# Layernorm statistics and gate rows moved from VectorE to ScalarE in a hybrid decoder step

## The chip, the cores and the metric

The kernel runs on all 8 cores of one Trainium2 chip. Each core works on its own share: one prompt sequence of 2048 tokens and 16 decode sequences of 8 tokens. The cores do not talk to each other. The time is that of the slowest core in device microseconds; the kernel before took 947.68 us in the median of three runs (946.88 to 950.29).

## The reference, cut to what matters

One layer of a decoder trunk. `a` is the normalised input, and `w_in` is one matrix whose columns are split into the inputs of two head groups.

```python
a = rmsnorm(h, norm_mix)
u, vg, q, k, vm, o, zi, zf = jnp.split(a @ w_in, SPLITS, axis=-1)
# head group A: chunked gMLP spatial gating (4 heads x 128 channels)
u = jax.nn.gelu(u)
vg = layernorm(jax.nn.gelu(vg), gm_ln_g, gm_ln_b)      # over the 512 channels of a token
y_gm = u * (causal 128x128 position mix of vg + bias)
# head group B: mLSTM matrix memory (4 heads, dk = dv = 128), chunks of 128 tokens
ig = zi + ml_b_i ; lf = log_sigmoid(zf + ml_b_f)
b  = cumsum(lf) ; m_t = running max of (b + m, b - b_s + ig_s)
w_inter = exp(b + m - m_t) ; w_end = exp(D[last] - m_new) ; dec = exp(b[last] + m - m_new)
num, den -> h ; C, n updated
...
h = h + [y_gm | y_ml] @ w_out
h = h + relu(rmsnorm(h) @ w_up)**2 @ w_down            # 1024 -> 4096 -> 1024
h = h + sigmoid(rmsnorm(h) @ w_pg) * (p @ w_pp) ; final rmsnorm
```

`layernorm` is `(x - mean) * rsqrt(var + eps) * g + b`, where mean and variance are over the 512 gMLP channels of a token. The outputs are the tokens, the new memories and the normalised `v` rows of the last chunk.

## The kernel before

**Tiles and halves.** A core has 17 tiles of 128 tokens: 16 of the prompt and one of the 16 decode sequences (the sample tile). They are worked on in two halves. The first holds prompt tiles 0 to 7 and the sample tile, in groups of two prompt tiles (256 columns), with the sample tile as a group of its own in third place. The second holds tiles 8 to 15 in four groups. A group goes through four stages: norm (`norm_T`, L865: square with accumulation and scaling on ScalarE, eight transposes on TensorE, one 128x1024 multiplication by the gain on VectorE, here `AR<-pb,GN`), projections (`stage_P`, L894: u, v, gates, o, m, q, k), the gate chain (`stage_G`, L958) and mixing (`stage_M`, L1047: both head groups, output projection, residual). When all groups of a half are through, the half's FFN follows in four quarters (`ffn_group`, L1169; its first matmuls are 128x384, three tiles wide), and the last per-layer step and the final norm (`stage_C`, L1189) follow the last quarter. The norms and the u, o and gate projections and the gate chain of the second half's first group stand before the last third of the first half's last FFN quarter.

**Layernorm of v, in `stage_P` (L934 to L945).** For each tile ScalarE evicts gelu of the v projection into `vn` (128x512, f32). VectorE takes its statistics in one pass and folds them (`bn_stats`, `bn_aggr`), GpSimd makes the reciprocal root (`rstd`, L861: a `tensor_scalar` and a power, 128x1 each), VectorE makes minus mean times that root (`stt`), ScalarE applies both (Identity with a bias and a scale of one number per partition), and GpSimd multiplies by the gain row `GROW` and adds the bias row `BROW` (128x512 each).

**The gate chain, in `stage_G` (L958 to L1030).** The gates lie as rows: 4 heads on 4 partitions, 256 tokens along the free axis. ScalarE makes exp and ln of the forget gate and adds the input gate's bias; VectorE makes the cumulative sum (`scan` into `ROWN`), adds it to the input gate, takes the running maximum (`scan` into `ROWR`), copies its value at the chunk ends into `RSEG`, and writes three blocks of rows into the tile `ROWX`, at partitions 32, 64 and 96: segment maximum minus running maximum, cumulative sum minus running maximum, and input gate minus segment maximum. TensorE transposes `ROWX` (matmuls `pb<-IDF,ROWX`, one per tile), spreads the decay of the memory (`pb<-DCB,ONEF`), and ScalarE exponentiates what comes out (`GSM`). `stage_M` cannot begin a tile without it. Matmuls `R,OH` spread the split running maximum.

**What sets the order.** Nothing is written out by hand. `stage_P`, `stage_G` and the others only record operations with their operands; a list scheduler (`Plan.schedule`, L393) gives each engine its order from estimated durations, from the cost of handing over between engines (`CROSS`, `SAME`), of changing ScalarE's function table (`TABLE`), and from how many PSUM banks each class of tiles may hold. So an edit of a few operations can move others far away. Where the scheduler foresees that TensorE will wait, it puts matmuls that compute nothing (`pb<-BSR,ONEB`, 128x512) before the waiting operation:

```python
spare = s - free[e] - 0.9 - (4.0 if late is not None and late.dma else 0.0)
each = FILL if s > 30.0 else 2 * FILL          # FILL = 0.22
o.fill = int(spare / each) if spare > 2 * each else 0
```

A single `BSR,ONEB` followed by `WM,AR x4` is no filler but the bias of the position mix. All instructions are issued from one helper line, L252, and all DMAs from L276, so the trace tells groups apart by tile names. Weights are loaded on GpSimd's queue: the FFN quarters by `load_q` (L1162), whose first quarter overlays the place of the u and v columns of `w_in`, so it is issued once the last group's u and v projections are through.

Of the kernel before, what the change touches and what calls it, by code (L numbers as in the profile page):

```python
# [7 lines left out]
AF = mybir.ActivationFunctionType  # L8
ALU = mybir.AluOpType
# [6 lines left out]
EPS = 1e-6  # L16
# [505 lines left out]
def build():  # L522
# [35 lines left out]
    with ExitStack() as st:  # L558
# [23 lines left out]
        def act(out, in_, func, bias=None, scale=None, accum=None):  # L582
            kw = dict(out=out, in_=in_, func=func)
            if bias is not None:
                kw["bias"] = bias
            if scale is not None:
                kw["scale"] = scale
            if accum is not None:
                kw["accum_out"] = accum
            cost = 0.17 + _nelem(in_) / 1200.0 + 0.09 * nptr(bias, scale) + (0.19 if accum is not None else 0)  # L590
            return P.add("act", [("activation", kw)], aps(in_, bias, scale), aps(out, accum), cost, tset=FN.get(func))
# [6 lines left out]
        def tt(eng, out, in0, in1, op):  # L598
            n = _nelem(out)
            mode = 2 if all(_dsize(x.dtype) == 2 for x in (out, in0, in1)) else 1  # L600
            cost = vcost(eng, n, mode)
            if eng == "pool":
                cost = 0.1 + n * (0.0026 if _dsize(in0.dtype) == 4 else 0.0019) + (0.55 if op == ALU.pow else 0)
            return P.add(eng, [("tensor_tensor", dict(out=out, in0=in0, in1=in1, op=op))], [in0, in1], [out], cost)

        def ts(eng, out, in0, s1, op0, s2=None, op1=None):
            kw = dict(out=out, in0=in0, scalar1=s1, scalar2=s2, op0=op0)
            if op1 is not None:
                kw["op1"] = op1
            mode = 1 if is_ps(in0) else (4 if _dsize(in0.dtype) == 2 and _dsize(out.dtype) == 2 else 2)  # L610
            return P.add(eng, [("tensor_scalar", kw)], aps(in0, s1, s2), [out],
                         vcost(eng, _nelem(out), mode, nptr(s1, s2)))

        def stt(eng, out, in0, scalar, in1, op0, op1):
            return P.add(eng, [("scalar_tensor_tensor", dict(out=out, in0=in0, scalar=scalar, in1=in1, op0=op0,
                                                             op1=op1))],
                         aps(in0, scalar, in1), [out], vcost(eng, _nelem(out), 1, nptr(scalar)))
# [8 lines left out]
        def dve(name, out, in_, **kw):  # L626
            return P.add("dve", [(name, dict(out=out, in_=in_, **kw))], [in_], [out], vcost("dve", _nelem(in_)))
# [129 lines left out]
        XH = [A.bf(512) for _ in range(3)]  # L757
# [100 lines left out]
        def small(g, off, n):  # L858
            return SMALL[:, g % 6, off:off + n]

        def rstd(out, tmp, ss, mul, add, n=1):  # L861
            ts("pool", tmp, ss, mul, ALU.mult, add, ALU.add)
            tt("pool", out, tmp, NEGH[:, 0:n], ALU.pow)
# [30 lines left out]
        def stage_P(grp, part=0, pg=None):  # L894
            gi = cnt["g"]
            nt = len(grp)
            n = nt * 128
            at = AT[gi % 2]
            d2 = gi % 2

            def feat(nm, fin):
                w = win(nm)
                for hp in range(2):
                    p = ps("P")
                    for hh in range(2):
                        h = hp * 2 + hh
                        mm(p[:, hh * n:(hh + 1) * n],
                           [(w[:, kc, h * 128:(h + 1) * 128], at[:, kc, 0:n]) for kc in range(8)])
                    fin(p[:, 0:2 * n].rearrange("p (h t) -> p h t", h=2), slice(hp * 2, hp * 2 + 2))

            def tokm(nm, j):
                w = win(nm)
                p = ps("P")
                mm(p, [(at[:, kc, j * 128:(j + 1) * 128], w[:, kc, :]) for kc in range(8)])
                return p

            marks = []
            if part == 2:
                marks = None
            else:  # L920
                feat("u", lambda p, hs: marks.append(act(UT[d2][:, hs, 0:n], p, AF.Gelu_apprx_tanh)))
            def gates():
                pg = ps("P")
                mm(pg[:, 0:n], [(WGT[:, kc, :], at[:, kc, 0:n]) for kc in range(8)])
                return pg

            def ogate():
                feat("o", lambda p, hs: act(SGT[d2][:, hs, 0:n], p, AF.Tanh, scale=0.5))

            if part == 1:  # L930
                pg = gates()
                ogate()
                return pg
            for j, t in enumerate(grp):  # L934
                vn = VN[t["n"] % 2]
                act(vn, tokm("v", j), AF.Gelu_apprx_tanh)
                st6, mv, tm, rs = small(t["n"], 4, 6), small(t["n"], 10, 2), small(t["n"], 12, 1), small(t["n"], 13, 1)
                dve("bn_stats", st6, vn)
                dve("bn_aggr", mv, st6)
                rstd(rs, tm, mv[:, 1:2], 1.0, EPS)  # L940
                nm = small(t["n"], 14, 1)
                stt("dve", nm, mv[:, 0:1], -1.0, rs, ALU.mult, ALU.mult)
                act(vn, vn, AF.Identity, bias=nm, scale=rs)
                tt("pool", vn, vn, GROW[:], ALU.mult)
                tt("pool", XH[t["n"] % 3], vn, BROW[:], ALU.add)  # L945
                if t["ty"] == 1 or t["i"] == NPT - 1:
                    tt("pool", vn, vn, BROW[:], ALU.add)
                    dma(o_Vs if t["ty"] == 1 else o_Vp, vn)
            if part == 0:
                pg = gates()  # L950
                ogate()
            for j, t in enumerate(grp):
                cp("act", VAUG[t["n"] % 4][:, :, 0:128], tokm("m", j).rearrange("p (h d) -> p h d", h=4))
            feat("q", lambda p, hs: cp("act", QT[d2][:, hs, 0:n], p))
            feat("k", lambda p, hs: act(KT[d2][:, hs, 0:n], p, AF.Copy, scale=QK_SCALE))
            return pg, marks

        def stage_G(grp, pg):  # L958
            gi = cnt["g"]
            d2 = gi % 2  # L960
            nt = len(grp)
            n = nt * 128
            ty = grp[0]["ty"]
            X = ROWX[d2]
            aa, L, NB, RR = X[0:4, 0:n], ROWL[0:4, 0:n], ROWN[0:4, 0:n], ROWR[0:4, 0:n]
# [26 lines left out]
                rs0, rs1 = rseg[:, 0:16], rseg[:, 16:32]  # L992
            v3 = lambda a: a.rearrange("p (s t) -> p s t", t=sl)
            bc = lambda a: a.unsqueeze(2).to_broadcast([4, nseg, sl])
            tt("dve", v3(X[32:36, 0:n]), bc(rs0), v3(RR), ALU.subtract)
            tt("dve", X[64:68, 0:n], NB, RR, ALU.subtract)
            tt("dve", v3(X[96:100, 0:n]), v3(aa), bc(rs1), ALU.subtract)
            r3 = R3[d2]
            act(r3[0:4, 0:n], RR, AF.Copy, scale=-1.0)
            rl_ = ROWL[32:36, 0:n]  # L1000
# [419 lines left out]
```

## Time and profile before

| | before |
|---|---|
| median of three runs | 947.68 us (946.88 to 950.29) |
| the profiled execution | 946.88 us |
| its span on the slowest core (core 0) | 945.3 us |
| spans of the eight cores | 942.1 to 945.3 us |
| TensorE (PE) busy | 896.8 us, 95% |
| VectorE (DVE) busy | 563.0 us, 60% |
| ScalarE (ACT) busy | 403.6 us, 43% |
| GpSimd (POOL) busy | 265.7 us, 28% |

The span is the time from the first to the last instruction of one core in the profiled execution; the execution's own time is 1.6 us longer. Busy shares are means over stages: a TensorE at 95% over the whole can still wait in some stages, and the stages are in this order: norms, projections and mixing of the first half until about 200 us, FFN until about 550 us, the second half's mixing until about 650 us, its FFN and the end. `PEclk` is the clock that was granted to TensorE, as a share of full speed (2.4 GHz); the other level is 0.5 (1.2 GHz).

### The profile page before, as it was taken

The numbers are of one execution on the slowest core, as the hardware profiler recorded it, in microseconds if no ns is written. First come the engines' busy times: TensorE is split into PE (matmuls) and PEld (weight loads), VectorE is DVE, ScalarE is ACT, GpSimd is POOL, SyncE is SP. The second block draws the span as 40 slices with busy tenths as digits, with TensorE's granted clock in tenths as the row PEclk, the third lists the DMA queues.
The fourth block names the chain that finished last, engine by engine and source line by source line (L and its number), as shares of the span: only waits on it lengthen the run. The fifth ranks groups of instructions, "written<-read, shape, count | busy, mean of one in ns | idle before, by whom it ended". The sixth has DMA issues, their size and how long they took to land.

```text
span 945.3 us, 17332 instructions; the slowest of 8 cores (942.1 to 945.3 us)
## 1 busy us (share of the span) xinstructions
PE 896.8 (95%) x5958; PEld 536.2 (57%) x5958; DVE 563.0 (60%) x1059; ACT 403.6 (43%) x742; POOL 265.7 (28%) x371
## 2 busy tenths in 40 slices
PE   6869899999999999999999999999999999999994
PEld 3547567665555555555456657667556555655552
DVE  2385955798555555435664696678744444445664
ACT  3446646664112122125467685476412211225453
POOL 3553434752111010001132374557300000001211
PEclk8879999999999999999999999999999999999998
DMA  8993235796979275292349210019999629000111
GB/s 182 170 197 45 68 23 59 109 170 128 162 135 177 68 129 95 55 166 57 111 106 196 57 68 1 1 21 169 129 119 171 115 30 149 1 12 23 52 45 67
DMA packets 64494, 90.70 MB, mean 96 GB/s; under 512 B 12550, under 2 KB 31882, under 8 KB 64408
## 3 DMA queue, kind: packets, MB, share of 16 engines
q0 software_dynamic: 37472, 59.51, 42.9%
q1 hardware_dynamic: 26936, 30.09, 10.8%
q8 instruction: 49, 0.80, 0.4%
q14 instruction: 37, 0.30, 0.1%
HBM read 133.59 MB, written 13.93 MB: 156 GB/s over the span
## 4 chain that ended last, share of the span: by engine, by line
PE 81%; DVE 5%; issue 4%; ACT 4%; DMA 2%; POOL 2%; DVEq 0%; POOLq 0%; ACTq 0%
PE pb L252 81%; ACT AR L252 3%; DVE AR L252 2%; DMA AR<-w_v 2%; POOL SMALL L252 1%; DVE SMALL L252 1%; DVE ROWX L252 1%; POOL AR L252 1%; ACT L252 1%; DVE H L252 1%; DMA H<-xp 0%; ACT ROWL L252 0%; POOL CSTB L252 0%; DVE BSR L252 0%; DVE ROWR L252 0%
## 5 line engine op out<-in xcount | busy, mean ns | idle before, releaser
L252 PE MATMUL pb<-AR 128*128 128x512 bf16 (+4 forms) x4924 | 827.6, 327 | 12.9 <-DMA AR<-w_v 4.5
L252 PEld LDWEIGHTS pb<-AR 128*128 128x128 bf16 x4924 | 466.0, 99 | 341.1 <-issue 24.4
L252 ACT ACTIVATE AR<-pb 128x384 f32<-128x384 f32 (+5 forms) x349 | 175.0, 512 | 402.8 <-PE pb L252 336.7
L252 DVE TENSOR_TENSOR H<-H,pb 128x512 f32<-128x512 f32 x170 | 116.7, 686 | 130.8 <-PE pb L252 130.1
L252 DVE TENSOR_TENSOR AR<-AR 128x384 bf16<-128x384 f32 (+1 forms) x192 | 107.3, 562 | 99.8 <-ACT AR L252 99.8
L252 ACT ACTIVATE AR<-H 128x1024 bf16<-128x1024 f32 x68 | 71.6, 1053 | 42.3 <-DVE H L252 26.9
L252 DVE TENSOR_TENSOR AR<-pb,GN 128x1024 bf16<-128x1024 bf16 x51 | 61.8, 1217 | 28.2 <-PE pb L252 28.0
L252 POOL TENSOR_TENSOR SMALL<-SMALL,NEGH 128x1 f32<-128x1 f32 (+1 forms) x102 | 67.3, 661 | 39.8 <-DVE SMALL L252 26.8
L252 POOL TENSOR_SCALAR SMALL<-SMALL 128x1 f32<-128x1 f32 x85 | 24.2, 285 | 192.5 <-ACT AR L252 148.7
L252 ACT ACTIVATE AR<-H,SMALL 128x1024 bf16<-128x1024 f32 x51 | 57.9, 1145 | 30.5 <-POOL SMALL L252 29.9
L252 PE MATMUL pb<-IDB,AR 128*128 128x128 bf16 x578 | 47.9, 220 | 14.0 <-ACT AR L252 7.4
L252 DVE SCALAR_TENSOR_TENSOR AR<-AR,pb 128x512 f32<-128x512 f32 (+1 forms) x51 | 34.8, 684 | 37.3 <-PE pb L252 22.5
L252 PEld LDWEIGHTS pb<-IDB,AR 128*128 128x128 bf16 x578 | 38.1, 98 | 27.6 <-issue 19.8
L252 DVE TENSOR_TENSOR AR<-pb,AR 128x258 f32<-128x258 f32 (+2 forms) x85 | 47.0, 576 | 3.8 <-PE pb L252 1.5
L276 POOL DMA_DIRECT2D AR<-w_up x8 | 7.5, 937 | 123.0 <-PE pb L252 122.8
L252 POOL CAST AR<-AR 128x256 bf16<-128x256 f32 x17 | 7.7, 453 | 118.7 <-PE pb L252 87.4
L252 ACT ACT_TABLE_LOAD x25 | 32.1, 1283 | 7.5 <-DMA H<-xp 5.3
L252 POOL TENSOR_TENSOR AR<-KTOKS,SEQ 128x1024 bf16<-128x1024 bf16 x8 | 15.1, 1891 | 57.1 <-PE pb L252 57.1
L252 PE MATMUL pb<-BSR,ONEB 128*128 128x512 bf16 x85 | 25.8, 420 | 3.4 <-DVE BSR L252 2.6
L252 ACT ACTIVATE AR<-AR 128x512 f32<-128x512 f32 x34 | 21.1, 628 | 16.2 <-DVE AR L252 11.7
L252 DVE SCALAR_TENSOR_TENSOR AR<-H,SMALL,AR 128x1024 f32<-128x1024 f32 x17 | 22.7, 1336 | 5.8 <-POOL SMALL L252 5.6
L252 ACT ACTIVATE AR<-pb,GSM 128x129 f32<-128x129 f32 x68 | 21.2, 365 | 10.8 <-PE pb L252 7.7
(105 smaller groups left out, 479.9 us busy)
## 6 DMA issues: line engine op xcount, KB each, us to landing
AR<-w_up POOLq DMA_DIRECT2D x8, 2048.0 KB, 19.6
AR<-w_down POOLq DMA_DIRECT2D x8, 2048.0 KB, 21.9
y_p<-AR SPq DMA_DIRECT2D x16, 512.0 KB, 3.1
H<-xp SPq DMA_DIRECT2D x14, 512.0 KB, 5.7
AR<-w_out POOLq DMA_DIRECT2D x2, 2048.0 KB, 35.8
AR<-sC SPq DMA_DIRECT2D x8, 512.0 KB, 4.7
AR<-w_pg POOLq DMA_DIRECT2D x2, 2048.0 KB, 30.9
o_Cs<-AR SPq DMA_DIRECT2D x8, 512.0 KB, 10.5
```

Of the source, the lines that this page charges most:

```text
L252: ins = getattr(e, name)(**kw)
L276: lambda e, out=out, in_=in_, sem=sem, kw=kw: e.dma_start(out=out, in_=in_, **kw).then_inc(sem, 16))
```

## The change

Two pieces of work leave VectorE. In `stage_P` the eviction gelu(v) also accumulates the sum of its row (`s1`), GpSimd turns it into minus the mean times a constant (`mc`), a second ScalarE pass squares the centred row and accumulates the variance (`vr`; its elementwise result goes into a buffer that is overwritten afterwards, `XH`), and GpSimd makes root and bias. In `stage_G`, for groups of prompt tiles alone, two of the three `ROWX` blocks are written by ScalarE, tile by tile (4x128 each, with the segment maximum as the bias), with one small VectorE operation that negates the segment maximum. The sample tile's gate chain stays.

```diff
             for j, t in enumerate(grp):
                 vn = VN[t["n"] % 2]
-                act(vn, tokm("v", j), AF.Gelu_apprx_tanh)
-                st6, mv, tm, rs = small(t["n"], 4, 6), small(t["n"], 10, 2), small(t["n"], 12, 1), small(t["n"], 13, 1)
-                dve("bn_stats", st6, vn)
-                dve("bn_aggr", mv, st6)
-                rstd(rs, tm, mv[:, 1:2], 1.0, EPS)
-                nm = small(t["n"], 14, 1)
-                stt("dve", nm, mv[:, 0:1], -1.0, rs, ALU.mult, ALU.mult)
+                s1, mc, vr, rs, nm, tm = (small(t["n"], o_, 1) for o_ in (4, 5, 6, 7, 8, 9))
+                c_ = 512 ** -0.5
+                act(vn, tokm("v", j), AF.Gelu_apprx_tanh, accum=s1)
+                ts("pool", mc, s1, -c_ / 512, ALU.mult)
+                act(XH[t["n"] % 3], vn, AF.Square, bias=mc, scale=c_, accum=vr)
+                rstd(rs, tm, vr, 1.0, EPS)
+                ts("pool", nm, mc, 1.0 / c_, ALU.mult, rs, ALU.mult)
                 act(vn, vn, AF.Identity, bias=nm, scale=rs)
...
-            tt("dve", v3(X[32:36, 0:n]), bc(rs0), v3(RR), ALU.subtract)
+            if ty == 0:
+                nr = rseg[:, 36:36 + nt]
+                ts("dve", nr, rs1, -1.0, ALU.mult)
+                for j in range(nt):
+                    tk = slice(j * 128, (j + 1) * 128)
+                    act(X[32:36, tk], RR[:, tk], AF.Identity, bias=rs0[:, j:j + 1], scale=-1.0)
+                    act(X[96:100, tk], aa[:, tk], AF.Identity, bias=nr[:, j:j + 1])
+            else:
+                tt("dve", v3(X[32:36, 0:n]), bc(rs0), v3(RR), ALU.subtract)
+                tt("dve", v3(X[96:100, 0:n]), v3(aa), bc(rs1), ALU.subtract)
             tt("dve", X[64:68, 0:n], NB, RR, ALU.subtract)
-            tt("dve", v3(X[96:100, 0:n]), v3(aa), bc(rs1), ALU.subtract)
```

The counts that follow over the whole program: VectorE loses 17 `bn_stats`, 17 `bn_aggr`, 17 small products and 16 of the `ROWX` operations and gains 8 operations on 4x2; ScalarE gains 17 squares of 128x512, 17 more reads of an accumulator at the gelu and 17 at the squares, and 32 operations on 4x128; GpSimd gains 34 `tensor_scalar` of 128x1. The fillers go from 68 to 75.

The scheduler then gives three engines another order. In the fences below, names are the kernel's tiles: `pb` is PSUM, `H` the residual, `AR` the arena that holds weights and activations, `SMALL` per-token numbers, `CSTB` the memory C.

On ScalarE at the start of the first half, from the evictions of the first group's projections on (before; the five evictions in the first row are u, v and o of group 0):

```order
L252 ACTIVATE AR<-pb 128x512 x5
L252 ACTIVATE AR<-AR,SMALL 128x512 x2
L252 ACTIVATE ROWX<-pb,GBI 4x256
L252 ACTIVATE AR<-pb 128x512
L252 ACTIVATE ROWL<-pb,GBI 4x256
L252 ACTIVATE ROWL<-ROWL 4x256
L252 ACTIVATE AR<-pb 128x512 x2
L252 ACTIVATE ROWX<-pb,GBI 4x256
L252 ACTIVATE R_0<-ROWR 4x256
L252 ACTIVATE AR<-pb 128x512 x2
L252 ACTIVATE ROWL<-pb,GBI 4x256
```

The same place after (`AR,SMALL<-AR,SMALL` is the square with accumulation, `ROWX<-ROWR,RSEG` and `ROWX<-ROWX,RSEG` the new gate rows):

```order
L252 ACTIVATE AR<-pb 128x512
L252 ACTIVATE AR,SMALL<-AR,SMALL 128x512 x2
L252 ACTIVATE ROWX<-pb,GBI 4x256
L252 ACTIVATE AR<-pb 128x512
L252 ACTIVATE AR<-AR,SMALL 128x512 x2
L252 ACTIVATE ROWL<-pb,GBI 4x256
L252 ACTIVATE ROWL<-ROWL 4x256
L252 ACTIVATE AR,SMALL<-pb 128x512 x2
L252 ACTIVATE ROWX<-ROWR,RSEG 4x128 x2
L252 ACTIVATE AR<-pb 128x512
L252 ACTIVATE ROWX<-ROWX,RSEG 4x128 x2
L252 ACTIVATE R_0<-ROWR 4x256
```

Two squares now stand between the o evictions and the exponential of the gates (`ROWL<-pb,GBI`), and the gate rows of group 0 stand behind the gelu evictions of group 1.

On TensorE in the same stretch, before; the second `IDF,ROWX` is the gate transposition of group 1:

```order
L252 MATMUL pb<-AR 128x256 x8
L252 MATMUL pb<-R_0,OH 128x128 x4
L252 MATMUL pb<-AR 128x512 x16
L252 MATMUL pb<-BSR,ONEB 128x512
L252 MATMUL pb<-WM,AR 128x128 x4
L252 MATMUL pb<-AR 128x256 x16
L252 MATMUL pb<-IDF,ROWX 128x128 x2
L252 MATMUL pb<-AR 128x256 x32
L252 MATMUL pb<-CSTB,AR 128x129 x2
```

After, the same place:

```order
L252 MATMUL pb<-AR 128x256 x8
L252 MATMUL pb<-R_0,OH 128x128 x4
L252 MATMUL pb<-AR 128x512 x16
L252 MATMUL pb<-R_0,OH 128x128 x4
L252 MATMUL pb<-AR 128x256 x16
L252 MATMUL pb<-AR 128x512 x8
L252 MATMUL pb<-AR 128x256 x32
L252 MATMUL pb<-CSTB,AR 128x129 x2
```

and, 40 rows further down, where it stands now:

```order
L252 MATMUL pb<-AR 128x512 x8
L252 MATMUL pb<-AR 128x128 x16
L252 MATMUL pb<-AR 128x512 x16
L252 MATMUL pb<-IDF,ROWX 128x128 x2
L252 MATMUL pb<-AR 128x128 x8
L252 MATMUL pb<-DCB,ONEF 128x8
```

Group 1's gate transposition moved behind the projections of both groups and the first mixing stage.

On TensorE where the second half's last mixing stage meets its FFN, before (`IDB,AR` are transposes, 128x384 are FFN matmuls):

```order
L252 MATMUL pb<-IDB,AR 128x128 x2
L252 MATMUL pb<-BSR,ONEB 128x512
L252 MATMUL pb<-WM,AR 128x128 x4
L252 MATMUL pb<-IDB,AR 128x128 x4
L252 MATMUL pb<-AR 128x384 x8
L252 MATMUL pb<-AR 128x129 x4
L252 MATMUL pb<-R_0,OH 128x128 x4
L252 MATMUL pb<-AR 128x128 x4
L252 MATMUL pb<-AR 128x129 x4
L252 MATMUL pb<-AR 128x384 x8
L252 MATMUL pb<-AR 128x129 x4
L252 MATMUL pb<-AR 128x384 x16
```

After:

```order
L252 MATMUL pb<-CSTB,AR 128x129 x2
L252 MATMUL pb<-IDB,AR 128x128 x8
L252 MATMUL pb<-CSTB,AR 128x129 x2
L252 MATMUL pb<-AR 128x129 x4
L252 MATMUL pb<-BSR,ONEB 128x512 x6
L252 MATMUL pb<-AR 128x129 x4
L252 MATMUL pb<-IDB,AR 128x128 x4
L252 MATMUL pb<-BSR,ONEB 128x512 x3
L252 MATMUL pb<-AR 128x512 x16
L252 MATMUL pb<-IDB,AR 128x128 x16
L252 MATMUL pb<-AR 128x384 x16
```

Before, 32 FFN matmuls lie between the pieces of the last mixing stage; after, nine fillers do, and the first FFN matmul comes behind the whole stage.

## Rows read from the trace of the kernel before

**Rows 1.** The page's parts 1 and 4: engines, and the chain that ended last

```profile
PE 896.8 (95%) x5958; PEld 536.2 (57%) x5958; DVE 563.0 (60%) x1059; ACT 403.6 (43%) x742; POOL 265.7 (28%) x371
PE 81%; DVE 5%; issue 4%; ACT 4%; DMA 2%; POOL 2%; DVEq 0%; POOLq 0%; ACTq 0%
```

**Rows 2.** Busy time by stretch of the span; first line names the columns

```profile
core 0: us, PE busy (x) PEld busy (x) DVE busy (x) ACT busy (x) POOL busy (x), PEclk, DMA share, GB/s
66.00:72.00 6.00, 6.00 (x33) 4.32 (x32) 2.19 (x7) 0.85 (x3) 1.64 (x2) 0.55 1.08 168
...
88.00:125.00 37.00, 31.87 (x330) 21.88 (x328) 35.54 (x80) 23.45 (x48) 17.92 (x24) 1.00 0.14 44
...
552.00:558.00 6.00, 4.54 (x53) 3.50 (x49) 5.64 (x13) 5.37 (x11) 5.17 (x8) 1.00 0.22 90
558.00:564.00 6.00, 5.25 (x25) 2.21 (x24) 5.93 (x14) 5.16 (x8) 3.38 (x7) 0.72 0.01 3
...
651.00:657.00 6.00, 4.98 (x53) 3.48 (x51) 6.00 (x12) 5.63 (x14) 5.75 (x8) 1.00 1.09 172
```

**Rows 3.** What TensorE waited for, 0 to 80, 80 to 230, 560 to 700 us: total, times, longest

```profile
PE pb L252 <- DVE ROWX L252: 7.3, 2, 4.1
...
PE pb L252 <- DVE AR L252: 5.8, 11, 1.4
...
PE pb L252 <- DVE AR L252: 1.4, 3, 0.6
```

**Rows 4.** TensorE's timeline: start, us, operation, in brackets idle time before and releaser

```profile
50.99 0.66 PE L252 MATMUL pb<-IDF,ROWX 128*128 128x128 f32 x2 [3.20 <-DVE ROWX L252]
...
65.62 0.66 PE L252 MATMUL pb<-IDF,ROWX 128*128 128x128 f32 x2 [4.15 <-DVE ROWX L252]
66.07 6.27 PE L252 MATMUL pb<-AR 128*128 128x256 bf16 x32
...
155.19 1.46 PE L252 MATMUL pb<-BSR,ONEB 128*128 128x512 bf16 x6
...
559.58 1.87 PE L252 MATMUL pb<-BSR,ONEB 128*128 128x512 bf16 x4
...
663.47 4.70 PE L252 MATMUL pb<-AR 128*128 128x384 bf16 x25
```

**Rows 5.** VectorE's timeline, the same gate row operation in two groups

```profile
61.21 1.45 DVE L252 TENSOR_TENSOR ROWX<-RSEG,ROWR 4x256 f32<-4x256 f32 x1
...
645.02 0.41 DVE L252 TENSOR_TENSOR ROWX<-RSEG,ROWR 4x256 f32<-4x256 f32 x1
```

**Rows 6.** ScalarE's timeline, an eviction of group 0's projections

```profile
37.44 0.60 ACT L252 ACTIVATE AR<-pb 128x512 bf16<-128x512 f32 x1 [1.15 <-PE pb L252]
```

**Rows 7.** GpSimd's timeline beside group 1's gate rows

```profile
61.13 2.66 POOL L252 TENSOR_TENSOR AR<-AR,GROW 128x512 f32<-128x512 f32 x2
```

**Rows 8.** Groups by operation and shape: count | busy us, mean ns | idle before

```profile
L252 DVE BATCH_NORM_STATS2 SMALL<-AR 128x6 f32<-128x512 f32 x17 | 11.7, 686 | 13.2 <-ACT AR L252 13.1
L252 DVE BATCH_NORM_AGGREGATE SMALL<-SMALL 128x2 f32<-128x6 f32 x17 | 3.0, 178 | 0.9
L252 DVE SCALAR_TENSOR_TENSOR SMALL<-SMALL 128x1 f32<-128x1 f32 x17 | 5.1, 306 | 4.4 <-POOL SMALL L252 4.4
L252 DVE TENSOR_TENSOR ROWX<-RSEG,ROWR 4x256 f32<-4x256 f32 x8 | 4.4, 545 | 0.3
L252 ACT ACTIVATE AR<-AR 128x512 f32<-128x512 f32 x34 | 21.1, 628 | 16.2 <-DVE AR L252 11.7 <-DVE SMALL L252 3.3 <-DVE MPREV L252 0.6
L252 ACT ACTIVATION_READ_ACCUMULATOR AR<-H 128x1 f32 x68 | 12.9, 189 | 0.0
L252 ACT ACTIVATE ROWX<-pb,GBI 4x128 f32<-4x128 f32 x1 | 0.3, 343 | 0.0
L252 POOL TENSOR_SCALAR SMALL<-SMALL 128x1 f32<-128x1 f32 x85 | 24.2, 285 | 192.5 <-ACT AR L252 148.7 <-DVE SMALL L252 41.1 <-ACT R L252 0.3
```

**Rows 9.** The page's DMA issues: weights of an FFN quarter, median us to landing

```profile
AR<-w_up POOLq DMA_DIRECT2D x8, 2048.0 KB, 19.6
```

## The prediction

> **What bounds the kernel now.** I read the page's parts 1 and 4 first: TensorE is busy for 896.8 of 945.3 us and carries 81% of the chain that ended last; VectorE and ScalarE together carry 9% of it [rows 1]. So work taken from VectorE is worth only what TensorE waits for it. The second view is busy time by stretch, since 95% is a mean: in 88 to 125 us TensorE has 31.87 of 37 us and VectorE 35.54; at 552 to 564 TensorE lacks 2.2 us while VectorE is full, and at 651 to 657 it lacks 1.0 while VectorE is busy for all 6.00 [rows 2]. In these stretches of mixing VectorE is the engine that runs out. The third view is what TensorE waited for: 7.3 us in two waits for `ROWX`, the gate rows, before 80 us; 5.8 us in eleven waits for other VectorE results in 80 to 230; 1.4 us in three at the end of the second half's mixing [rows 3]. The fourth, its timeline, shows the two gate waits, 3.20 us before the transposition at 50.99 and 4.15 before the one at 65.62, and fillers at 155.19 and 559.58, which are waits that the scheduler filled [rows 4]. Behind the longer wait the 32 projection matmuls took 6.27 us: the granted clock of 66 to 72 us is 0.55, nearly all at the lower level, and at 558 to 564 it is 0.72 [rows 2, 4].
>
> **The change part by part.** I sum against the profiled execution, 946.88 us, which is 0.8 below the median of the runs shown.
>
> *Work moved.* VectorE loses 17 times 0.686 + 0.178 + 0.306 = 19.9 us of statistics and 16 gate operations of 0.545, 8.7 us: 28.6 in all, less eight tiny ones. Per group of two prompt tiles that is 2 x 1.17 + 2 x 0.545 = 3.4 us. ScalarE gains per such group two squares with their read (0.628 + 0.189), two reads at the gelu and four gate rows of about 0.343 (the nearest row, 4x128): 1.6 + 0.4 + 1.4 = 3.4 us, some 28 over the program. GpSimd gains 34 x 0.285 = 9.7 us [rows 8]. ScalarE is busy for 43% and GpSimd for 28% [rows 1], and in 88 to 125 us they have 23.45 and 17.92 of 37 us [rows 2], so as sums they are hidden; as links in a chain they are not, which is the first term below and the first rival.
>
> *Second gate wait, -6.8 (0 to -6.8).* In the order of after, group 1's gate transposition stands forty rows further down on TensorE, behind projections and the first mixing stage, some 30 us of its work later. So the wait of 4.15 us goes, and with it the slow clock behind it: 6.0 us at 0.55 cost 6.0 x 0.45 = 2.7 [rows 2, 4]. What is late next is the projections behind it, and their weights have landed by the time (TensorE runs them at once at 66.07).
>
> *First gate wait, +0.5 (0 to +1.5).* It stays. In the order of after two squares stand on ScalarE between the o evictions and the gates' exponential, 2 x 0.82 = 1.6 us at most; before one eviction there ScalarE was idle for 1.15 us, waiting for TensorE [rows 6], which covers most. The gate rows themselves cost 4 x 0.343 = 1.4 us on ScalarE against 2 x 0.545 on VectorE, about even [rows 8]. I take 0.5, the 1.6 less that idle time.
>
> *VectorE's relief in the first half, -3 (0 to -7).* Three and a half groups' worth, 4 x 3.4 = 13.6 us and the sample tile's 1.2, leave the mixing of the first half. The most that this can give back is what TensorE lost there: 5.8 us of waits and six fillers of 1.46 us, 7.3 [rows 3, 4]. The filler run isn't in the order of after; the eleven waits are short (longest 1.4) and many are latencies of one operation behind another, which a shorter queue does not remove. I take the fillers and a quarter of the waits.
>
> *The hole at 552 to 564, -4 (0 to -4.9).* Idle 1.46 + 0.75, four fillers 1.87, and about 0.8 for the real matmuls behind them at the low clock: 4.9 us [rows 2, 4]. The order of after has no fillers at that place, so I take all but the small waits.
>
> *New handovers in the second half, +2.5 (1 to 4).* The order of after has a run of three fillers behind the norms of its third group and a run of two in its second mixing stage, which before has not. Five fillers are at least 5 x 0.243 = 1.2 us (six took 1.46); a wait as long as the worst of before is 4.15 [rows 4]. I take the middle.
>
> *The seam to the last FFN, +5 (2 to 9).* Before, 32 FFN matmuls of 128x384 run between the pieces of the last mixing stage. At 4.70 / 25 = 0.188 us each [rows 4] they are 6.0 us of useful work under a stretch in which VectorE is full [rows 2], and TensorE waits only 1.4 us for it [rows 3]. After, that stage stands alone with nine fillers, because the norms in front of the FFN come behind both tiles on VectorE. The useful work is done later and costs its own time there; so the cover gone is about 6, less what VectorE's relief shortens: 5. At least it is the nine fillers, 2.2; at most the 6.0, the 1.4 not filled and the slow clock of a long hole, 0.8 as at 559: about 9 with rounding up.
>
> *First FFN weights, 0 (0 to +3).* `w_up` of the first half lands 19.6 us after its issue in the median [rows 9]. The order of after issues it with some 23 us of TensorE's work in hand, so it is hidden by 3; a landing later than that would cost what it exceeds.
>
> Sum: -6.8 + 0.5 - 3 - 4 + 2.5 + 5 + 0 = -5.8, that is 946.9 - 5.8 = 941.1 in a profiled execution like this one, or 941.9 beside the median.
>
> **A rule on the lock.** The same gate operation took 0.41 us at 645.02 and 1.45 at 61.21, where GpSimd was multiplying by `GROW` from 61.13 on [rows 5, 7]. The Trainium skill (SBUF — State Buffer, section "Who interferes with whom") has VectorE and GpSimd share one pair of ports under an exclusive lock, held for a whole instruction. The trace agrees, 1.04 us for one operation. By that rule the change removes two operations of a chain that can be held up, and adds 34 on GpSimd that can hold up others; where the chain meets `GROW` and `BROW` the seam would cost what the second rival says, and elsewhere nothing that the sum has not.
>
> **The rivals.** *No change, about 947.* The first-half gain comes back. Group 1's mixing now follows its late gate transposition at once, and ScalarE has gate rows, squares and evictions in one queue; a chain of exponential, scans, four gate rows, transposition and exponential again that is ready too late costs what it cost before, 4.15 us and the slow clock behind it, 6.8 [rows 2, 4], and the sum is +1. For it: ScalarE's part in the chain grows by four operations per group. Against it: the order of after puts 30 us of other work in front.
>
> *Slower, about 954.* At the seam, VectorE's last gate chain and last mixing stage run while GpSimd has `GROW` and `BROW` of the last tiles, which at 645.02 they did not (0.41 us). Some ten operations that touch SBUF alone would each take 1.0 us longer, as at 61.21 (1.45) [rows 5]. TensorE has no FFN matmuls to cover it now, so the seam costs 5 + 10, and the slow clock behind it 2.7 more [rows 2]: 941.1 + 12.7 = 953.8. It decides from the point where GpSimd's two multiplications start less than the chain's length ahead of it. For it: they did just that at 61 [rows 7], and GpSimd is busy for 5.75 of 6 us at 651 to 657 [rows 2]. Against it: a group's v is projected ahead of its o, m, q and k, so that both multiplications can be over when its gate chain is due, as they were at 645.
>
> *A larger gain, about 935.* VectorE really is what limits the mixing: all 7.3 us of the first half go instead of 3, and the seam costs 2, its lower end, because VectorE's part there is shorter as well: 941.1 - 4.3 - 3 = 933.8, or 934.6 beside the median.
>
> **How the numbers follow.** The forecast, 938 to 945 around 941.9, has 0.46; no change (946 to 949) 0.25; slower by the lock at the seam 0.16; the larger gain 0.13. A measurement of this kernel can tell about 0.5%, 4.7 us, from no change: faster is below 942.9, slower above 952.4. Of the forecast's 0.46 I put 0.37 below 942.9 and 0.09 within. Faster: 0.37 + 0.13 = 0.50; same: 0.09 + 0.25 = 0.34; slower: 0.16. The range of 8 in 10 reaches from the larger gain, 934, to 951, which leaves out most of the slower case and a little at the lower end.
>
> **What would show it.** In the timeline of after, no wait for `ROWX` near 65 us and a granted clock near 1 behind it (second gate wait); the wait near 51 us of 3 to 5 us (first); in 88 to 125 us TensorE busy for 33 or more of 37 and VectorE well below 35.5 (relief); no hole near 555; five fillers with short waits in the second half's mixing; and before the first 128x384 matmul of the second half a hole of 2 to 9 us in which VectorE is full and TensorE runs nine fillers. If VectorE's gate operations there read 1.4 us and not 0.4, the second rival is on. The forecast is wrong if the late gate transposition of group 1 is itself waited for by over 3 us, or if the seam costs over 9.

## The result and the profile after

The kernel after is slower: the profiled execution took 957.76 us against 946.88, and the ratio to the kernel before is 1.0105 (95% interval 1.0072 to 1.0138), some 10 us. Two of its four runs (about 974 us) showed a lower clock on one die and are left out of the ratio. The forecast was 941.9 us, the range 934 to 951: the time lies outside, and it moved the other way.

The page of after, its span and its engines, to be laid beside [rows 1]:

```profile
span 956.2 us, 17419 instructions; the slowest of 8 cores (950.9 to 956.2 us)
PE 898.2 (94%) x5965; PEld 536.3 (56%) x5965; DVE 536.1 (56%) x1000; ACT 424.2 (44%) x822; POOL 279.4 (29%) x405
```

VectorE lost 27 us of work, ScalarE gained 21 and GpSimd 14; counted were 28, 28 and 10 (ScalarE also has 22 table loads where it had 25). TensorE's busy time is the same to 1.4 us. So the 10 us are time in which TensorE waits.

To find where, I counted TensorE's own work in the order of its queue, by a convention: one column per cycle at 2.4 GHz, at least 0.0565 us for a small matmul, four times that for f32, and all `BSR,ONEB` matmuls (fillers and biases) left out (16 matmuls of 512 columns are 3.41 us by this and 3.61 in the timeline at 613.25, below). It is 847 us in every kernel here. What the trace's clock shows beyond it between two points of that work is lost time; the counted work is the same for all, so differences between kernels hardly depend on the convention. The medians over six cores with complete records (0, 1, 3, 5, 6 and 7 here), in us lost (the last two lines are of kernels that come further down):

| stretch of TensorE's work, us | up to 20 | 20 to 192, first half's mixing | 192 to 438, FFN | 438 to 505, second half begins | 505 to 597, rest of its mixing | 597 to 840, FFN | 840 to 847, end |
|---|---|---|---|---|---|---|---|
| before | 25.5 | 31.0 | 3.9 | 9.5 | 5.7 | 6.7 | 5.2 |
| after | 24.6 | 28.2 | 4.1 | 5.6 | 20.3 | 6.9 | 6.4 |
| late order of before | 26.7 | 27.7 | 4.1 | 11.6 | 6.0 | 7.0 | 5.8 |
| first half, gate rows alone | 26.0 | 28.0 | 3.6 | 9.3 | 5.8 | 6.7 | 5.8 |

After gains 2.8 us in the first half's mixing and 3.9 where the second half begins, and loses 14.6 in the rest of the second half's mixing and 1.2 at the end. The views say the same. Busy time by stretch of after (columns as in [rows 2]):

```profile
core 6: us, PE busy (x) PEld busy (x) DVE busy (x) ACT busy (x) POOL busy (x), PEclk, DMA share, GB/s
66.00:72.00 6.00, 6.00 (x51) 4.56 (x49) 0.00 (x0) 3.44 (x7) 4.08 (x4) 1.00 1.08 166
...
88.00:125.00 37.00, 32.69 (x288) 21.51 (x285) 26.58 (x64) 24.67 (x54) 20.80 (x25) 0.91 0.13 44
550.00:575.00 25.00, 24.61 (x203) 18.64 (x202) 3.20 (x4) 17.89 (x37) 11.44 (x22) 1.00 0.01 2
575.00:600.00 25.00, 22.15 (x169) 14.41 (x167) 21.73 (x52) 14.77 (x34) 9.32 (x11) 1.00 0.00 1
...
657.00:663.00 6.00, 3.98 (x44) 2.62 (x42) 6.00 (x14) 5.46 (x12) 3.31 (x7) 1.00 1.07 170
663.00:669.00 6.00, 4.12 (x24) 1.80 (x23) 5.67 (x15) 3.88 (x6) 2.37 (x4) 1.00 1.25 188
```

And of before, in the two stretches where the second half's mixing begins:

```profile
550.00:575.00 25.00, 22.63 (x155) 13.06 (x153) 23.53 (x52) 17.75 (x32) 15.91 (x23) 0.93 0.11 41
575.00:600.00 25.00, 25.00 (x219) 18.80 (x217) 13.88 (x33) 16.28 (x31) 13.23 (x16) 1.00 0.01 2
```

Before, VectorE has 23.53 of 25 us at 550 to 575, TensorE has its hole there, and is full after it. After, TensorE is full at 550 to 575 because it runs projections while VectorE has 3.20 us of work; the mixing that VectorE would have done stands behind. From 575 on TensorE runs short, to the last stage of mixing at 657 to 669, where it lacks 3.9 of 12 us.

What TensorE waited for in after, 565 to 650 us and then 650 to 672 (total, times, longest):

```profile
PE pb L252 <- DVE AR L252: 4.1, 5, 2.3
PE pb L252 <- DVE SMALL L252: 1.4, 1, 1.4
PE pb L252 <- ACT ROWL L252: 1.0, 1, 1.0
PE pb L252 <- DVE H L252: 0.8, 1, 0.8
PE pb L252 <- ACT AR L252: 0.6, 1, 0.6
PE pb L252 <- DVE CST L252: 0.5, 2, 0.3
PE pb L252 <- ACT GSM L252: 0.3, 1, 0.3
...
PE pb L252 <- ACT AR L252: 1.5, 2, 1.1
PE pb L252 <- DVE SMALL L252: 1.2, 2, 0.8
PE pb L252 <- DVE AR L252: 1.1, 3, 0.5
```

Of before, in 574 to 650, the same view has one line, and in 650 to 672 the last of [rows 3] (1.4 us):

```profile
PE pb L252 <- DVE RSEG L252: 0.9, 1, 0.9
```

That is 8.7 us in twelve waits against 0.9, and 3.8 us (with nine fillers, 2.3 more) against 1.4 at the seam to the FFN. TensorE's timeline of after shows how the second half's mixing looks now: a wait, a lump of projections, a wait, and at the end the fillers that were foreseen:

```profile
613.25 3.61 PE L252 MATMUL pb<-AR 128*128 128x512 bf16 x16 [1.39 <-DVE SMALL L252]
...
632.01 15.16 PE L252 MATMUL pb<-AR 128*128 128x256 bf16 x108
649.43 0.38 PE L252 MATMUL pb<-IDB,AR 128*128 128x128 bf16 x4 [2.25 <-DVE AR L252]
...
662.17 1.46 PE L252 MATMUL pb<-BSR,ONEB 128*128 128x512 bf16 x6
...
665.66 0.81 PE L252 MATMUL pb<-BSR,ONEB 128*128 128x512 bf16 x3
666.93 3.61 PE L252 MATMUL pb<-AR 128*128 128x512 bf16 x16 [0.46 <-DVE AR L252]
...
671.28 2.76 PE L252 MATMUL pb<-AR 128*128 128x384 bf16 x16
```

At the start of the first half the wait at 65 us is gone, the clock at 66 to 72 is 1.00, and the first gate wait is longer than before (5.53 against 3.20 us):

```profile
53.30 0.57 PE L252 MATMUL pb<-DCB,ONEF 128*128 128x8 f32 x2 [5.53 <-DVE DCB L252]
```

VectorE's timeline in front of it:

```profile
42.55 5.54 DVE L252 CAST BSR<-AR 1x512 bf16<-1x512 f32 x1
48.02 0.67 DVE L252 TENSOR_TENSOR_SCAN ROWN<-ROWL,ZROW 4x256 f32<-4x256 f32 x1
```

and GpSimd's:

```profile
42.86 2.51 POOL L252 TENSOR_TENSOR AR<-AR,GROW 128x512 f32<-128x512 f32 x2
45.31 2.49 POOL L252 TENSOR_TENSOR AR<-AR,BROW 128x512 bf16<-128x512 f32 x2
```

A small cast that takes 0.42 us elsewhere lasted 5.54, from before GpSimd's four operations on 128x512 until after them, and the gate chain's first scan stood behind it. The clock that was slow at 66 to 72 is now slow behind this longer wait, and once more near 100 us (columns as above):

```profile
54.00:58.00 4.00, 4.00 (x23) 2.94 (x22) 2.17 (x6) 2.52 (x7) 2.24 (x4) 0.50 1.02 255
...
100.00:104.00 4.00, 3.68 (x11) 1.51 (x12) 0.00 (x0) 3.89 (x8) 3.66 (x3) 0.50 0.00 0
```

Near 100 us TensorE waits for ScalarE. The layernorm of a tile stands there on ScalarE until GpSimd has its numbers, and the eviction that TensorE needs stands behind it in ScalarE's queue. GpSimd, ScalarE and TensorE of after:

```profile
94.89 2.31 POOL L252 TENSOR_SCALAR SMALL<-SMALL 128x1 f32<-128x1 f32 x1 [1.06 <-ACT AR L252]
...
99.09 0.81 ACT L252 ACTIVATE AR<-AR,SMALL 128x512 f32<-128x512 f32 x1 [3.11 <-POOL SMALL L252]
...
100.32 11.17 PE L252 MATMUL pb<-AR 128*128 128x512 bf16 x56 [3.66 <-ACT AR L252]
```

### The profile page after: what moved, and what is told of

It reads as the page before. It is cut to its first block, busy times and chain, and to the rows that moved or that the text cites. A ratio compares the mean times of both kernels' runs of the same rounds, so it can differ in the third digit from the quotient of the medians.

```text
span 956.2 us, 17419 instructions; the slowest of 8 cores (950.9 to 956.2 us)
## 1 busy us (share of the span) xinstructions
PE 898.2 (94%) x5965; PEld 536.3 (56%) x5965; DVE 536.1 (56%) x1000; ACT 424.2 (44%) x822; POOL 279.4 (29%) x405
## 4 chain that ended last, share of the span: by engine, by line
PE 82%; DVE 5%; issue 4%; ACT 3%; DMA 3%; POOL 2%; SPq 0%; POOLq 0%; DVEq 0%; ACTq 0%
PE pb L252 82%; ACT AR L252 3%; DVE AR L252 2%; POOL SMALL L252 2%; DMA H<-xp 2%; DMA AR<-wsT 1%; DVE SMALL L252 1%; DVE H L252 0%; SPq L276 0%; ACT L252 0%; DVE BSR L252 0%; DVE ROWX L252 0%; DVE ROWR L252 0%; DVE CST L252 0%; ACT ROWX L252 0%
## 5 line engine op out<-in xcount | busy, mean ns | idle before, releaser
L252 POOL TENSOR_SCALAR SMALL<-SMALL 128x1 f32<-128x1 f32 x119 | 35.7, 300 | 192.7 <-ACT AR L252 179.6
L252 ACT ACTIVATE AR<-H,SMALL 128x1024 bf16<-128x1024 f32 x51 | 58.2, 1145 | 28.1 <-POOL SMALL L252 27.7
L252 PE MATMUL pb<-IDB,AR 128*128 128x128 bf16 x578 | 47.6, 221 | 14.6 <-ACT AR L252 8.0
L252 DVE TENSOR_TENSOR AR<-pb,AR 128x512 bf16<-128x512 f32 (+2 forms) x85 | 46.9, 577 | 10.5 <-PE pb L252 7.8
L252 ACT ACT_TABLE_LOAD x22 | 28.2, 1283 | 11.2 <-DMA H<-xp 5.7
L252 PE MATMUL pb<-BSR,ONEB 128*128 128x512 bf16 x92 | 28.4, 425 | 4.6 <-DVE BSR L252 2.6
L252 ACT ACTIVATE AR<-AR,SMALL 128x512 bf16<-128x512 f32 (+1 forms) x34 | 25.8, 764 | 13.0 <-POOL SMALL L252 12.4
L252 POOL TENSOR_TENSOR AR<-AR,BROW 128x512 bf16<-128x512 f32 (+1 forms) x19 | 25.2, 1328 | 1.7
```

The source lines that it names most:

```text
L252: ins = getattr(e, name)(**kw)
```

## Experiments

Two questions: is it the new operations, or the order that the scheduler made of them? And if the operations, which?

**One half of the change each.** The layernorm part of the diff alone, and the gate part alone, each ordered anew by the scheduler.

> The layernorm statistics by accumulating activations alone; the gate rows stay on VectorE. The scheduler orders everything anew. Theory A (the order that the scheduler makes decides, the operations themselves are nearly free): the time is that of another order, anywhere in 945 to 960, and what it loses against before stands in holes of TensorE in one mixing stage, not spread over the groups. Theory B (the longer chain through ScalarE and GpSimd per tile decides, or the square's result in the buffer XH, which has to wait for an older tile's mixing): at least half of the 10 us, 952 to 956, and every group's v chain is longer. Theory C (the four gate rows per group on ScalarE decide): 945 to 948, no slower than before.

> The gate rows on ScalarE alone; the statistics stay on VectorE. Theory A (order): another order, anywhere in 945 to 960. Theory B (statistics): 945 to 948. Theory C (gate rows: four operations of about 0.4 us in ScalarE's queue in every prompt group's gate chain): 952 to 957, with TensorE waiting for the gate transposition or for what follows it in most groups.

Measured: the statistics alone 1.0417 of before (1.0388 to 1.0447; profiled 988.23 us), the gate rows alone 1.0130 (1.0103 to 1.0157). Neither half is better than the whole, and the statistics alone are four times worse than both together. No theory of a price per operation gives that: 1.3% and 4.2% don't add up to 1.05%. By the table's measure both lose in the same stretch as after (505 to 597: 20.3 and 25.0 us), and the statistics alone 18.1 us in the last FFN where before loses 6.7. There, and on the slowest cores of the gate rows alone, GpSimd waited for late loads of `pp` (see the last section). Each is a different order with other waits for transfers; as tests of the operations they are inconclusive.

**Operations and order apart.** So I fixed the order. The scheduler's choice is replaced by a table of the operations in the order wanted, with fillers and PSUM banks:

```diff
     def schedule(self, caps):
         ops = self.ops
+        order = []
+        for (i, f, bs) in FIXED:
+            o = ops[i]
+            o.fill = f
...
+                p.bank = b
+            order.append(o)
+        return order
```

> All operations of after, but in the order that the scheduler gave before: each engine's order, the PSUM banks and the fillers are a fixed table, the new operations stand where the ones that they replace stood, on their new engine (one square has to wait for a later place, since its buffer is still read). Theory A (order): 940 to 948, no slower than before, because VectorE is relieved by 28 us and no other thing moved; the FFN matmuls cover the last mixing stage again and the second half's mixing (575 to 675 us) loses some 6 us, not 20. Theories B and C (operations): 953 to 960, about the time of after.

> All operations of before, in the order that the scheduler gave after, again as a fixed table with banks and fillers. Theory A (order): 955 to 965, about the time of after or above it, since VectorE has its 28 us more as well; 575 to 675 us loses some 14 us more than before. Theories B and C (operations): 945 to 950, the time of before.

Measured: new operations in the old order 1.0106 (1.0091 to 1.0122), old operations in the new order 1.0269 (1.0238 to 1.0300). My expectation for the first was wrong as a total: it is as slow as after. But it is slow elsewhere:

| us lost | 20 to 192 | 438 to 505 | 505 to 597 |
|---|---|---|---|
| before | 31.0 | 9.5 | 5.7 |
| new operations, old order | 37.6 | 12.4 | 5.6 |
| old operations, new order | 32.4 | 6.6 | 24.1 |
| after | 28.2 | 5.6 | 20.3 |

The ratio 1.0269 goes by the slowest cores, 2 and 5 (977 and 973 us, the others 958 to 963), where GpSimd also waited 12.4 and 10.1 us for a load of `pp` before the last FFN; the medians leave most of that out. The last column goes by the order, whatever the operations: 5.7 and 5.6 in the old, 24.1 and 20.3 in the new. In the first half the operations count, and in both signs: put where the old ones stood they cost 6.6 us, in the order made for them they save 4.2 (28.2 against 32.4).

**The order of the second half alone.** In the middle of the first half's FFN both orders have done exactly the same work, so they can be joined there.

> All operations of after. Up to the middle of the first half's FFN, a point at which both orders have done exactly the same work, the order that the scheduler gave after; from there on the order that it gave before (fixed table, the new operations where the replaced ones stood). Theory A1 (the slowdown is the order of the second half's mixing stages alone): the 505 to 597 us of TensorE's own work lose 6 us again and not 20, everything before is as in after, and the whole comes to within 4 us of before, some 8 below after. Theory A2 (the new operations cost their time wherever they stand): no more than 3 us below after.

Measured: 0.9987 (0.9977 to 0.9997), 1.2% less than after's ratio; the stretch 505 to 597 lost 6.0 us. All that after loses against before is the order of the second half: order, banks and fillers of all engines together. Which move in it does it is read from the views above and not tested by itself. TensorE's waits in this kernel, 574 to 672 us (core 6), where after has the 12.5 us of its two lists above:

```profile
PE pb L252 <- DVE AR L252: 1.8, 4, 0.6
PE pb L252 <- DVE RSEG L252: 0.8, 1, 0.8
PE pb L252 <- ACT AR L252: 0.5, 1, 0.5
```

and busy time at 550 to 600, where the hole of before is back and TensorE is full after it:

```profile
550.00:575.00 25.00, 20.37 (x142) 11.50 (x140) 20.59 (x43) 20.91 (x39) 15.80 (x24) 1.00 0.06 23
575.00:600.00 25.00, 24.98 (x217) 18.63 (x216) 10.96 (x24) 17.38 (x37) 14.24 (x20) 1.00 0.01 2
```

**Why the new operations cost in the old order.** The square's unused result goes into `XH`, which an older tile's mixing may still have to read.

```diff
+        JK = A.bf(512)
...
-                act(XH[t["n"] % 3], vn, AF.Square, bias=mc, scale=c_, accum=vr)
+                act(JK if t["n"] < 9 else XH[t["n"] % 3], vn, AF.Square, bias=mc, scale=c_, accum=vr)
```

> As the run with all operations of after in the order of before, but in the first half the square's unused result goes to a buffer of its own instead of XH, so that no square has to wait for the matmuls of an older tile's mixing. Theory D (that wait in ScalarE's queue is what the new operations cost in the old order): the loss at 120 to 165 us of TensorE's work falls from 12 to about 6 us, and the whole is 4 to 6 us faster than that run. Theory E (the longer chain of the statistics over ScalarE and GpSimd, eviction, mean, square, root, bias): within 2 us of that run.

Its four runs lie between 957.91 and 1033.44 us and give no ratio; the profiled one, 957.99 us, lies 1.2 below the profiled run that it is compared with (959.15). In the trace 20 to 192 lost 35.3 us against 37.6, and 100 to 192, where the wait should have been, 12.9 against 13.8. So that wait is not it, at most about a third of the 6.6 us. By the sign set down before the run (within 2 us) the rest falls to the longer chain; whether it is the chain or a bad fit of chain and order stays open.

**Is before's order an ordinary one?** One constant of the scheduler changed by a hundredth, in both kernels.

```diff
-CROSS, SAME = 0.22, 0.06
+CROSS, SAME = 0.21, 0.06
```

> Before, with one constant of the scheduler changed by a hundredth (the handover between engines, 0.22 to 0.21): the same operations in another order. Theory A (the order is a draw, and before's is a lucky one): 5 to 20 us slower than before. Theory F (before's order is typical, and the change made it worse for a reason of its own): within 4 us of before.

> After, with the same constant at 0.21. Theory A: another draw, as likely faster as slower than after, by 5 us or more, and not 10 us slower than before with the same constant. Theory F: some 10 us slower than before with the same constant.

Measured: before 1.0222 (1.0174 to 1.0270), after 1.0146 (1.0115 to 1.0178), both against before as it was. The same operations as before cost 21 us more in a neighbouring order, twice what the change cost, and with this constant the kernel with the change is the faster by 0.7%, on two and three runs and with intervals that touch.

**The scheduler's own best draws.** Three constants drawn at random some hundred times for each kernel, and the draw taken that the scheduler's own estimate rates best.

> After, with three constants of the scheduler (handover, margin of TensorE, table change) at 0.164, 0.46 and 1.14, the draw that the scheduler itself rates best of some hundred. If the order is what decides and the scheduler's rating is worth something: 935 to 948, 10 to 20 us faster than after. If the rating misses what the chip adds (waits for transfers above all): anywhere in 945 to 970.

> Before, with the same three constants at 0.188, 0.39 and 1.19, rated best of as many draws for the operations of before. If the order decides: 935 to 948, and within 5 us of the best draw of after, since the change itself then is worth only a few us. If the change were bad for a reason of its own, the best draw of after would be some 10 us slower than this.

Measured: after 1.0206 (1.0184 to 1.0227), before 1.0010 (0.9992 to 1.0028). Both were expected at 935 to 948 us if the scheduler's estimate is worth something, and neither came there. By the sign written down before, the best draw of after some 10 us slower, this pair speaks for a change that is bad for a reason of its own: it is 19 us slower. It doesn't settle it, since each is another order and in after's draw the last FFN loses 15.6 us (before's draw 11.9, before 6.7), up to 25.2 on core 6, where GpSimd waited for a transfer (see the last section). Against a reason of its own stands the run with the late order of before, which has all operations of after at 0.9987.

**The change where it pays.** The change in the first half alone, with the order and operations of before from the middle of the FFN on, and then without the statistics:

```diff
-                act(vn, tokm("v", j), AF.Gelu_apprx_tanh)
...
+                if t["n"] < 9:
+                    s1, mc, vr, rs, nm, tm = (small(t["n"], o_, 1) for o_ in (4, 5, 6, 7, 8, 9))
...
-            if ty == 0:
+            if ty == 0 and grp[0]["n"] < 9:
```

> The change in the first half alone: the operations and the order of after up to the middle of the first half's FFN, from there on the operations and the order of before (fixed table). If the new operations gain in the first half what the traces show there (2 to 5 us of TensorE's waiting less at 192 us of its work) and cost in the second half, in before's order, what the trace of the run with the late old order shows (2 to 3 us), this is 2 to 5 us faster than before and 1 to 3 faster than that run: a ratio of 0.995 to 0.998. If the second half's part of that cost is only noise between cores, it equals that run, 0.9987.

> As the run with the change in the first half alone, with the gate rows on ScalarE, but with the statistics back on VectorE at the places of the new operations, in the same order (fixed table); from the middle of the first half's FFN on all is as in before. If the gain of the first half comes from the statistics (VectorE's relief of 1.17 us a tile): 1.000 to 1.003 of before, 2 to 5 us slower than that run. If it comes from the gate rows, or from the order alone: 0.996 to 0.999, as that run.

Measured: 0.9977 (0.9967 to 0.9988), and with the gate rows alone 0.9959 (0.9946 to 0.9973, median 945.54 us against 949.17 on that chip). This last one beats both kernels. It differs from "old operations, new order" in the first half by the gate rows only, and loses 28.0 us there and not 32.4; with the statistics moved too the three kernels that have this order lost 28.2, 27.7 and 29.3. That looks as if the statistics did nothing, though in this half they are 10.5 us (9 tiles of 1.17) of the 15 taken from VectorE, and the gate rows 4.4. Split by stretch (medians by the same count), they do two things that cancel:

| us lost | 20 to 40 | 40 to 66 | 66 to 192 |
|---|---|---|---|
| before | 12.3 | 5.0 | 13.7 |
| old operations, new order | 8.5 | 9.5 | 14.2 |
| first half, gate rows alone | 8.1 | 7.0 | 13.0 |
| gate rows and statistics (after; late order of before; first half new) | 8.3; 8.4; 9.2 | 9.0; 8.2; 8.9 | 11.1; 11.1; 11.1 |

The gate rows bring 0.4, 2.5 and 1.2 us in the three stretches. The statistics bring 1.9 in the last and cost 0.2 to 1.1 in the first and 1.2 to 2.0 in the middle one, where TensorE waits 3.6 to 3.7 us for ScalarE near 100 us on every core of after, of the late order of before and of the first half new. With the statistics on VectorE the same wait is 1.27 (core 3 of the gate rows alone):

```profile
97.63 4.51 PE L252 MATMUL pb<-AR 128*128 128x512 bf16 x32 [1.27 <-ACT AR L252]
```

So the chain of the statistics over ScalarE and GpSimd costs at this one handover what it gives back later. That GpSimd's link in it, 2.31 us for an operation of 0.2 to 0.5 beside a multiplication on VectorE, is the lock from the other side is not tested.

## Why the prediction was wrong, by its steps

- **Second gate wait, -6.8: right where it stood, given back in part beside it.** The wait is gone and the clock at 66 to 72 is 1.00. But the slow clock moved behind the longer first wait: 0.50 at 54 to 58 us, where before has 0.96 (core 0; in the 4 us ahead of that it has 0.62 and after 0.67). The stretch of work that holds both gate waits, 20 to 40, went from 12.3 us lost to 8.3: -4.0 for both terms together, against -6.3.
- **First gate wait, +0.5 (0 to +1.5): it was +2.3,** outside its bounds; on the eight cores it is 4.98 to 6.36 us. Not the squares did it: with the operations of before in this order it is 4.8 to 6.0 us as well. Beside it stand GpSimd's multiplications and additions, 42.86 to 47.80, and a VectorE operation of 5.54 us; six of the eight cores show one of 5.5 to 5.95 there. That the lock held it up is inferred from the two times. I had the lock, with its price for one operation, and placed it at the wrong end of the kernel. The Trainium skill (SBUF — State Buffer, section "Who interferes with whom") has the lock held for one instruction; here the waiting operation got in only behind four in a row, so a price per instruction is too low by about that factor where GpSimd's queue is full.
- **No term: +4.0 in the stretch of work from 40 to 66** (5.0 to 9.0 us lost). The sum held the longer chain of the statistics to be hidden except at the first gate wait; near 100 us it is not, and TensorE waits 3.66 us for ScalarE, with the slow clock behind it. The nearest that was written down is the rival of no change, which had ScalarE's queue as the limit, though for the gate transposition.
- **VectorE's relief, -3 (0 to -7): -2.6,** from 66 to 192 us of work (13.7 to 11.1). The size is about right; with the order held, 1.2 are the gate rows' and 1.9 the statistics' (against 14.2 with the operations of before in this order). The 13.6 us named there are those of four groups, not of three and a half; the term doesn't hang on it.
- **The hole at 552 to 564, -4: right, -3.9** (438 to 505: 9.5 to 5.6), **but a loan.** The hole went because projections were run early; I did not ask what VectorE did meanwhile (little, 3.20 of 25 us) and where its mixing would come.
- **New handovers in the second half, +2.5 (1 to 4): +7.8 in waits alone** (8.7 against 0.9). This is the step that failed. By the count of lost time, 505 to 597 lost 14.6 us more, where this term and the seam together had 7.5, and the same operations in before's late order lose 6.0 there. I priced what the order shows, five fillers, and took one long wait as the upper end. But the scheduler puts a filler only where it foresees a wait; most of the twelve, of 0.2 to 2.3 us, it did not foresee, and they show in no order. What the order did show, and I read past, is that the projections stand in lumps (108 matmuls without a break at 632) and no longer between the steps of the mixing; that it is these lumps, among all that is new in this order, is read and not tested.
- **The seam, +5 (2 to 9): right,** 3.8 + 2.3 against 1.4, +4.7. So neither of the two signs came by which the forecast was to be known as wrong: the seam cost under 9, and group 1's gate transposition was not waited for. It failed where no sign had been set.
- **First FFN weights, 0: right** (192 to 438: 3.9 and 4.1). The last 7 us of work lost 1.2 more; I had nothing there.

The sum of steps was -5.8; with the measured sizes (-2.8 for the first half, -3.9, +14.6, +1.2) it is +9. The slower rival named about the right time, 954, by luck, since its reason was wrong: in the last gate chain only a scan and an addition were held up (1.40 and 1.24 us at 640 to 643, some 1.6 more than usual), not ten operations. The rival of a larger gain did not come: the relief gave 2.6 and not 7.3, and the seam cost 4.7 and not 2. The fault behind all of it is one: I summed local gains of an order, as if the rest stayed, when the whole order was new. The prediction gave "some other place gets worse" two terms of 7.5 us with narrow bounds, while a neighbouring order of the unchanged kernel costs 21.

## What to carry to other kernels

Where a scheduler orders a kernel, an edit is first a new draw of the order; measure the spread of draws of the unchanged kernel before any size is given to an edit, and test the edit with the order held fixed. A hole that goes because independent work was run earlier is a loan: look for the stretch that loses that cover. Relieving a crowded engine pays only as far as the chain that the work moves into isn't waited for: in the order of after the first half's gate rows, 4.4 us of VectorE's work, were worth 4.4 us, and its statistics, 10.5 us, gave back 1.9 and cost as much at one handover.

## What the runs showed of the hardware

VectorE did not get in between GpSimd's operations: 5.54 us for a cast of 0.42, in after on core 6, and on core 3 the same for the operation before it in VectorE's queue, which takes 0.65 to 0.69 us otherwise:

```profile
38.93 5.55 DVE L252 TENSOR_TENSOR WM<-AR 128x512 bf16<-128x512 f32 x1 [2.02 <-DMA AR<-wsT]
```

And a small transfer that lands late can stop a whole core. In the best draw of after, on core 6, one of the last 128 KB loads of `pp` took 21.9 us to land while FFN weights were on the way; the quickest took 2.1. What SyncE waited for at 655 to 700 us, and the landing times of the loads from 600 on:

```profile
SPq L235 <- DMA AR<-pp: 23.7, 3, 19.7
...
DMA to landing us min/median/max: 2.1/8.1/21.9
```

GpSimd's cast stood waiting for it, and the norm behind it on GpSimd held up ScalarE and TensorE (GpSimd's timeline):

```profile
690.11 0.40 POOL L252 CAST AR<-AR 128x256 bf16<-128x256 f32 x1 [16.75 <-DMA AR<-pp]
```

TensorE waited 13.73 us for it, and busy time by stretch, with the columns of [rows 2], has every engine empty in 682 to 690.

```profile
692.42 1.01 PE L252 MATMUL pb<-IDB,AR 128*128 128x128 bf16 x8 [13.73 <-ACT AR L252]
...
682.00:686.00 4.00, 0.00 (x0) 0.00 (x0) 0.00 (x0) 0.00 (x0) 0.00 (x0) 0.50 0.63 40
686.00:690.00 4.00, 0.00 (x0) 0.00 (x0) 0.00 (x0) 0.00 (x0) 0.00 (x0) 0.50 0.90 94
```

Other runs show it too. With the statistics alone, cores 4 and 5, whose waits for `pp` were the longest (17.8 and 17.0 us), lost 24.1 and 26.3 us in that FFN, and core 7 (4.9 us) 7.5; in before no core waited longer than 4.9, and 6.7 were lost. With the gate rows alone the slow cores 1, 3 and 5 (962 to 965 us) waited 9.4, 6.9 and 8.5 us for such a load, cores 2, 4 and 7 (950 to 951) 2.6, 4.7 and 2.7. A program's time is that of its slowest core, so these ratios hold landing times as well as the change.
